# A transformer stack on one core: full-column fillers among the one-column mean-square products of three norms

## The chip, the cores and the metric

The kernel runs on one core of one Trainium2 chip. The metric is the time of one execution on the device in microseconds; the number given for a kernel is the median of several executions.

## The reference

The input x has 256 tokens of 1024 features, in float32. Two layers of a first block (root-mean-square norm with a modulation, a wide input projection, three kinds of attention with gates, output projections, a second norm and a residual) are followed by a second block: a norm and a recurrent/forgetting-attention mixer ("mix" 0), a norm and a feed-forward part ("ffn" 0), a norm and a gated linear attention ("mix" 1), a norm and a mixture of experts ("ffn" 1), and a last norm. What matters here is the norm, which stands at every one of these joints:

```
def rms_norm(x, g):
    xf = x.astype(jnp.float32)
    y = xf * lax.rsqrt(jnp.mean(xf * xf, axis=-1, keepdims=True) + EPS)
    return (y * g.astype(jnp.float32)).astype(x.dtype)
```

## The kernel before

x lies on the chip transposed, features on the 128 partitions, in KD = 8 groups k of 128 features by S = 256 tokens; a token's mean square is therefore a sum over partitions and over k, and TensorE makes it. Each engine has its own list of instructions, written out by hand in one order, and the engines meet only at semaphores; TensorE's order is that of the code in its block.

At a norm the steps are these. VectorE finishes x, two k at a time (L2439 and L2443 after a layer of the first block, L2614 after the feed-forward part). ScalarE squares it, two k at a time, into `sq` (`pair_squares`, L1471). TensorE multiplies each square, as the stationary operand, with one column of a matrix that holds 1/1024: `token_square` (L654), two matmuls per k (one for each 128 tokens) of a single output column each, all summed in one bank of the accumulators; `token_squares` (L660) does this for all eight k, waiting before each for its square. ScalarE takes the root (L1516), VectorE the reciprocal (`inverse_tokens`, L2145), and `spread` (L667) turns the 2 columns of reciprocals into 128 equal rows over 256 tokens with two matmuls against the identity. VectorE multiplies h with them (L2313, L2472). In the projections that follow, h is needed as two parts of lower precision, upper and lower, which ScalarE (L1593, L1506) and VectorE (L2317, L2476) form; a product of two such operands is three matmuls (`product`, L693 to L698).

`keep_busy(n)` (L676) puts n matmuls of 128 by 128 by 128 into a bank of the attention group, whose result nobody reads. It waits for whatever frees the bank whose turn it is, but it claims no turn. It stands between the mean squares and the spread, where TensorE waits for the root, and between the spread and the projection, where it waits for h. A float32 matmul appears in the trace as two records.

`token_squares` is called at three places: the norm "pre" of the second layer (L896), "mix" 0 (L1014) and "mix" 1 (L1146). Elsewhere the mean squares are made between other products. After "pre" 1 comes a projection of two targets (`project`, L699 on), after "mix" 0 the forget gate's product with h (`chunk`, L643, 16 records), after "mix" 1 a product with 16 columns (the same helper).

Of the kernel before, what the change touches and what calls it, by code (L numbers as in the profile page):

```python
# [83 lines left out]
class Ticks:  # L84
# [12 lines left out]
    def when(self, sem, *step):  # L97
        return self.known.get((sem.name, *step), 1)


def two_blocks(nc, A, C, out, known):

    _, S, D = A["x"].shape
    L = A["w_in"].shape[0]
    KD, NT = D // P, S // P
    FF = A["ev_ffn_w1_2"].shape[2]
    NE, _, FE = A["od_exp_w1_2"].shape[1:]
    SLOT, RING = 2048, 6
    ticks = Ticks(known)
# [279 lines left out]
    def cols(name, l, a, b, k=None):  # L389
# [6 lines left out]
    ADA_SPREAD = {("gcols", 0, 0): (1, 2), ("gcols", 0, 3): (1, 3), ("gcols", 0, 8): (1, 1),  # L396
                  ("gcols", 1, 0): (1, 4), ("gcols", 1, 3): (1, 5)}
    ADA_UNITS = [(0, 0), (0, 1), (0, 2)] + [u for _, u in ADA_LATER.items()]
    ADA_SLOW = [u for _, u in ADA_SPREAD.items()]

# [126 lines left out]
    def wrote(*key):  # L527
        tick(psum_ready, *key)
        return 1
# [81 lines left out]
    def _(pe):  # L611
# [4 lines left out]
        def claim(group, key, freed_by, *step):  # L616

            n = order[group][turn[group] % 4]
            turn[group] += 1
            if n in busy:  # L620
                pe.wait_ge(busy[n][0], busy[n][1])
            busy[n] = (freed_by, when(freed_by, *step))
            ticks.counts[("bank", *key)] = n
            return bank[n]
# [29 lines left out]
        def token_square(b, at, tile, k, scale, start, stop):  # L654
            for t in range(NT):
                m = nc.tensor.matmul(b[:, at + t:at + t + 1], tile[:, k, P * t:P * t + P], mean[scale][:, 0:1],  # L656
                                     start=start and t == 0, stop=stop, skip_group_check=True)
            return m

        def token_squares(key):  # L660
            b = claim("gemm", ("ms", *key), rstd_ready, *key)
            for k in range(KD):
                pe.wait_ge(sq_ready, when(sq_ready, *key, k))
                m = token_square(b, 0, sq, k, 1024, k == 0, k == KD - 1)
            m.then_inc(psum_ready, wrote("ms", *key))

        def spread(key, first, n, freed_by, *step):  # L667

            pe.wait_ge(rstd_ready, when(rstd_ready, *key))
            b = claim("gemm", ("r", *key, first), freed_by, *step)  # L670
            for t in range(n):
                m = nc.tensor.matmul(b[:, P * t:P * t + P], rtok[:, first + t:first + t + 1].broadcast_to([P, P]), ident,
                                     start=True, stop=True)
            m.then_inc(psum_ready, wrote("r", *key, first))

        def keep_busy(n):  # L676

            b = order["attn"][turn["attn"] % 4]
            pe.wait_ge(*busy[b])
            for _ in range(n):  # L680
                nc.tensor.matmul(bank[b][:, 0:P], mean[1024], ident, start=True, stop=True)  # L681
# [209 lines left out]
        for l in range(L):  # L891
            if l == 0:
                for i in range(3):
                    modulation(0, i)
            else:
                token_squares(("pre", l))  # L896
                keep_busy(4)
                spread(("pre", l), 0, NT, h_ready, "pre", l, KD - 1)
                keep_busy(6)
# [112 lines left out]


        token_squares(("mix", 0))  # L1014
        keep_busy(4)
        spread(("mix", 0), 0, NT, h_ready, "mix", 0, KD - 1)
        keep_busy(5)
        pe.wait_ge(flog_spread, when(flog_spread, "all"))
        chunk(("flog",), "gemm", clog_ready, ("flog",), KD, lambda k: flogw[:, k], lambda k: h[:, k],
              fresh=("mix", 0))  # L1020
# [122 lines left out]
        for n in range(4):  # L1143
            busy[4 + n] = (x_ready, when(x_ready, "ffn", 2 * n + 1))

        token_squares(("mix", 1))  # L1146
        keep_busy(6)
        spread(("mix", 1), 0, NT, h_ready, "mix", 1, KD - 1)
# [1873 lines left out]
```

## Time and profile before

| | us |
|---|---|
| median of 3 executions | 2174.56 (2170.38 to 2179.92) |
| the profiled execution | 2178.82 |
| its span | 2177.0 |
| TensorE busy, matmuls | 2125.8 |
| VectorE busy | 1618.2 |
| ScalarE busy | 1273.3 |
| mean granted TensorE clock | 0.981 of full |

The span runs from the first to the last instruction in the profile; the device time of the same execution has 1.8 us around it. "PE" is TensorE's matmuls, "PEld" its weight loads, which overlap them. The granted clock is given as a share of 2.4 GHz, and 0.50 is the lower level, 1.2 GHz.

### The profile page before, as it was taken

To read this page: it belongs to the slowest core of one execution; us is meant where nothing else is said; L and a number is where in the kernel's file an instruction comes from. 1 tells how busy PE (TensorE), PEld (TensorE's weight loads), DVE (VectorE), ACT (ScalarE), POOL (GpSimd) and SP (SyncE) were. 2 spreads that over 40 slices of the span, in tenths; PEclk is the share of its full clock that TensorE was granted. 3 is DMA by queue.
4 is the path that set the end of the run, shared out by engine and by line. 5 is a ranking of instruction groups with operands and counts; after the bars stand their busy time and mean duration, and the time that the engine had idled before them with its cause. 6 is when DMAs were issued, how large, how long until landed. Compare 5 with 4: busy or idle time off the path is not lost.

```text
span 2177.0 us, 33231 instructions
## 1 busy us (share of the span) xinstructions
PE 2125.8 (98%) x12854; PEld 1904.0 (87%) x12854; DVE 1618.2 (74%) x1928; ACT 1273.3 (58%) x1546; POOL 26.7 (1%) x19
## 2 busy tenths in 40 slices
PE   6999999999999999999999999999999999999997
PEld 6899999999999989999998888888888888888886
DVE  6668866558855755555637888898898888888886
ACT  2645534645524744334635777777676777777675
POOL 0000000000000300000000000000000000000000
PEclk6999999999999999998999999999999999999999
DMA  9975355665435425554557999999999999999990
GB/s 287 238 239 184 120 173 118 161 188 180 117 117 171 145 88 176 190 160 140 156 189 283 374 343 353 357 347 376 334 365 341 362 347 351 376 331 368 335 352 29
DMA packets 361202, 536.48 MB, mean 246 GB/s; under 512 B 67724, under 2 KB 207936, under 8 KB 361096
## 3 DMA queue, kind: packets, MB, share of 16 engines
q1 hardware_dynamic: 355536, 530.81, 72.0%
q10 hardware_dynamic: 5560, 4.19, 0.7%
q8 instruction: 75, 1.23, 0.2%
q14 instruction: 31, 0.25, 0.0%
HBM read 533.89 MB, written 1.07 MB: 246 GB/s over the span
## 4 chain that ended last, share of the span: by engine, by line
PE 76%; DVE 3%; ACT 2%; issue 1%; DMA 0%; DVEq 0%; ACTq 0%
PE bank L696 21%; PE bank L698 21%; PE bank L697 21%; PE bank L643 3%; PE bank L1309 2%; PE bank L1264 1%; PE bank L1363 1%; ACT w_hi L1960 1%; PE bank L656 1%; PE bank L849 1%; DVE w_lo L2715 1%; PE bank L681 1%; DVE piece_lo L2452 1%; ACT piece_hi L1482 0%; PE bank L832 0%
## 5 line engine op out<-in xcount | busy, mean ns | idle before, releaser
L2715 DVE TENSOR_TENSOR w_lo<-pool,w_hi 128x2048 fp32r<-128x2048 f32 x336 | 765.1, 2292 | 101.3 <-ACT w_hi L1960 100.6
L1960 ACT ACTIVATE w_hi<-pool 128x2048 fp32r<-128x2048 f32 x336 | 643.0, 1917 | 135.4 <-PE bank L698 135.0
L696 PE MATMUL bank<-w_hi,xe_hi 128*128 128x512 f32 x896 | 356.2, 397 | 3.7 <-DVE h L2814 3.4
L698 PE MATMUL bank<-w_hi,xe_lo 128*128 128x512 f32 x896 | 349.7, 390 | 0.0
L697 PE MATMUL bank<-w_lo,xe_hi 128*128 128x512 f32 x896 | 349.1, 390 | 0.0
L696 PE MATMUL bank<-h_upper,upper 128*128 128x256 f32 x992 | 293.4, 296 | 3.2 <-DVE h_lo L2262 3.2
L697 PE MATMUL bank<-h_lo,upper 128*128 128x256 f32 x992 | 281.6, 284 | 0.0
L698 PE MATMUL bank<-h_upper,ring_lo 128*128 128x256 f32 x992 | 281.6, 284 | 0.0
L2172 DVE TENSOR_TENSOR ring_lo<-ring,upper 128x1024 fp32r<-128x1024 f32 x132 | 160.4, 1222 | 98.5 <-ACT upper L1493 98.0
L2452 DVE TENSOR_TENSOR piece_lo<-ring,piece_hi 128x1024 fp32r<-128x1024 f32 x118 | 144.9, 1236 | 100.4 <-ACT piece_hi L1482 100.1
L696 PEld LDWEIGHTS bank<-w_hi,xe_hi 128*128 128x128 f32 x896 | 168.2, 188 | 45.1 <-DVE h L2814 6.3
L698 PEld LDWEIGHTS bank<-w_hi,xe_lo 128*128 128x128 f32 x896 | 168.2, 188 | 36.1
L697 PEld LDWEIGHTS bank<-w_lo,xe_hi 128*128 128x128 f32 x896 | 168.5, 188 | 33.2
L696 PEld LDWEIGHTS bank<-h_upper,upper 128*128 128x128 f32 x992 | 190.9, 192 | 5.9 <-issue 4.1
L696 PE MATMUL bank<-left_hi,piece_hi 128*128 128x256 f32 x672 | 193.9, 289 | 0.8 <-DVE left_lo L2476 0.8
L697 PEld LDWEIGHTS bank<-h_lo,upper 128*128 128x128 f32 x992 | 191.0, 193 | 1.7 <-issue 0.2
L697 PE MATMUL bank<-left_lo,piece_hi 128*128 128x256 f32 x672 | 191.3, 285 | 0.0
L698 PE MATMUL bank<-left_hi,piece_lo 128*128 128x256 f32 x672 | 191.3, 285 | 0.0
L698 PEld LDWEIGHTS bank<-h_upper,ring_lo 128*128 128x128 f32 x992 | 190.8, 192 | 0.0
L696 PE MATMUL bank<-w_hi,hT_hi 128*128 128x512 f32 x448 | 176.0, 393 | 0.0
L698 PE MATMUL bank<-w_hi,hT_lo 128*128 128x512 f32 x448 | 174.5, 389 | 0.0
L697 PE MATMUL bank<-w_lo,hT_hi 128*128 128x512 f32 x448 | 174.3, 389 | 0.0
(396 smaller groups left out, 3427.0 us busy)
## 6 DMA issues: line engine op xcount, KB each, us to landing
pool<-in_od_exp_w SPq DMA_DIRECT2D x336, 1024.0 KB, 7.2
ring<-in_w_in SPq DMA_DIRECT2D x48, 1024.0 KB, 5.4
ring<-in_ev_ffn_w SPq DMA_DIRECT2D x33, 1024.0 KB, 5.3
ring<-in_w_ada SPq DMA_DIRECT2D x24, 1024.0 KB, 7.2
ring<-in_od_w_in SPq DMA_DIRECT2D x12, 1024.0 KB, 5.6
ring<-in_ev_w_in SPq DMA_DIRECT2D x10, 1024.0 KB, 5.4
ring<-in_w_in SPq DMA_DIRECT2D x32, 256.0 KB, 4.6
ring<-in_w_out SPq DMA_DIRECT2D x8, 1024.0 KB, 5.1
```

The lines of the kernel that those rows point to most:

```text
L643: m = nc.tensor.matmul(b[base:base + rows, 0:cols], left(k), right(k), start=(k == 0), stop=(k == K - 1))
L656: m = nc.tensor.matmul(b[:, at + t:at + t + 1], tile[:, k, P * t:P * t + P], mean[scale][:, 0:1], start=start and t == 0, stop=stop, skip_ ...
L681: nc.tensor.matmul(bank[b][:, 0:P], mean[1024], ident, start=True, stop=True)
L696: nc.tensor.matmul(b, left[0], right[0], start=first, stop=False, skip_group_check=True)
L697: nc.tensor.matmul(b, left[0], right[1], start=False, stop=False, skip_group_check=True)
L698: return nc.tensor.matmul(b, left[1], right[0], start=False, stop=last, skip_group_check=True)
L849: m = nc.tensor.matmul(b[:, 0:S], v[:, k, at:at + P], pT[:, k], start=(k == 0), stop=(k == NT - 1))
L1309: m = nc.tensor.matmul(bank[n][:, P * c:P * c + P], h_tok[:, t, P * (4 * g + c):P * (4 * g + c) + P], pick_tok[:, t], start=(t == 0), stop ...
L1960: nc.scalar.activation(w_hi[q % 3], ring_slot(q), ACT.Copy)\
L2172: V.tensor_tensor(dst, src, split(upper[:, n % PIECES], KD, P).bitcast(F32), ALU.subtract)\
L2452: V.tensor_tensor(lo, src, hi.bitcast(F32), ALU.subtract).then_inc(piece_ready, tick(piece_ready, n))
L2715: V.tensor_tensor(w_lo[q % 3], ring_slot(q), w_hi[q % 3].bitcast(F32), ALU.subtract)\
```

## The change

Inside `token_squares`, ahead of the products of k = 2, 4 and 6, three unread full-column matmuls are issued: nine per call, at three calls. And the fillers between the spread and the forget gate's product at "mix" 0 go from five to eight.

```
@@ -661,6 +661,8 @@
             b = claim("gemm", ("ms", *key), rstd_ready, *key)
             for k in range(KD):
                 pe.wait_ge(sq_ready, when(sq_ready, *key, k))
+                if k in (2, 4, 6):
+                    keep_busy(3)
                 m = token_square(b, 0, sq, k, 1024, k == 0, k == KD - 1)
             m.then_inc(psum_ready, wrote("ms", *key))
 
@@ -1014,7 +1016,7 @@
         token_squares(("mix", 0))
         keep_busy(4)
         spread(("mix", 0), 0, NT, h_ready, "mix", 0, KD - 1)
-        keep_busy(5)
+        keep_busy(8)
```

## Rows read from the trace of the kernel before

**Rows 1.** The page: span, busy time, and the chain that ended last by engine.
```profile
span 2177.0 us, 33231 instructions
...
PE 2125.8 (98%) x12854; PEld 1904.0 (87%) x12854; DVE 1618.2 (74%) x1928; ACT 1273.3 (58%) x1546; POOL 26.7 (1%) x19
...
PE 76%; DVE 3%; ACT 2%; issue 1%; DMA 0%; DVEq 0%; ACTq 0%
```

**Rows 2.** Windows around the norms: stretch, length, PE busy, PEclk, DMA share, GB/s.
```profile
366.90:371.00 4.10, 3.85 (x32) 1.00 0.00 1
...
372.10:375.40 3.30, 3.05 (x15) 0.50 0.00 0
...
679.10:682.80 3.70, 3.37 (x27) 0.98 0.54 170
682.90:689.50 6.60, 6.60 (x30) 0.50 0.39 110
...
1004.80:1006.90 2.10, 2.10 (x22) 1.00 0.03 8
1007.00:1013.70 6.70, 6.70 (x33) 0.50 0.00 0
```

**Rows 3.** Chain at "mix" 1: start us, us on the chain, what.
```profile
1004.90 4.65 PE bank L656 x32
1009.54 2.77 PE bank L681 x12
1012.31 0.85 PE bank L672 x4
1013.17 1.69 PE bank L681 x12
1014.85 3.56 PE bank L643 x16
```

**Rows 4.** Chain at "mix" 0.
```profile
681.51 2.54 PE bank L656 x16
684.05 1.92 PE bank L681 x8
685.97 0.85 PE bank L672 x4
686.82 2.13 PE bank L681 x10
688.95 3.79 PE bank L643 x16
```

**Rows 5.** Timeline at "mix" 0: start us, us, engine, line, what, [idle before <-releaser].
```profile
680.31 0.97 PEld L656 LDWEIGHTS bank<-mean,sq 128*128 128x128 f32 x8 [0.17 <-ACT sq L1471]
...
681.51 2.46 PEld L656 LDWEIGHTS bank<-mean,sq 128*128 128x128 f32 x16 [0.23 <-ACT sq L1471]
```

**Rows 6.** Timeline at "pre" 1.
```profile
368.02 0.97 PEld L656 LDWEIGHTS bank<-mean,sq 128*128 128x128 f32 x8 [0.17 <-ACT sq L1471]
...
369.22 1.86 PEld L656 LDWEIGHTS bank<-mean,sq 128*128 128x128 f32 x16 [0.23 <-ACT sq L1471]
...
371.06 1.22 DVE L2172 TENSOR_TENSOR ring_lo<-ring,upper 128x1024 fp32r<-128x1024 f32 x1
...
374.99 0.88 DVE L2317 SCALAR_TENSOR_TENSOR h_lo<-h,small,h_upper 128x256 fp32r<-128x256 f32 x2
```

**Rows 7.** One-column products amid other work: the chain, and the window around it.
```profile
620.75 1.68 PE bank L656 x16
...
618.00:624.20 6.20, 6.20 (x38) 5.68 (x37) 1.90 (x5) 1.74 (x3) 0.00 (x0) 1.00 0.52 169
```

**Rows 8.** Chain at "pre" 1.
```profile
372.41 1.22 PE bank L672 x4
373.63 2.27 PE bank L681 x12
```

**Rows 9.** Window after "mix" 1: length, five engines' busy time, PEclk, DMA share, GB/s.
```profile
1024.00:1031.00 7.00, 7.00 (x32) 6.35 (x31) 1.31 (x2) 1.73 (x5) 0.00 (x0) 0.51 0.83 260
```

More of the change, by code:

```diff
@@ L663, in token_squares @@
                 pe.wait_ge(sq_ready, when(sq_ready, *key, k))
+                if k in (2, 4, 6):
+                    keep_busy(3)
                 m = token_square(b, 0, sq, k, 1024, k == 0, k == KD - 1)
@@ L1016, in _ @@
         spread(("mix", 0), 0, NT, h_ready, "mix", 0, KD - 1)
-        keep_busy(5)
+        keep_busy(8)
         pe.wait_ge(flog_spread, when(flog_spread, "all"))
```

## The prediction

> **What bounds the kernel now.** I read the page first: the shares of busy time and the chain that ended last. TensorE (PE) is busy for 98% of a 2177.0 us span and carries 76% of the chain; no other engine has more than 3% [rows 1]. So a microsecond added to or taken from PE's own order counts in full, unless PE stands waiting at that point. Then I cut the span into short windows and looked at the granted clock around the three norms that the diff touches ("pre" of layer 1, "mix" 0, "mix" 1). In each the clock goes from 1.00 to 0.50, the lower of its two levels (1.2 GHz where 2.4 is full), and stays there: about 3.3 us at pre 1, 6.7 us at mix 0, 6.8 us at mix 1 [rows 2]. What PE did just before is the same each time: the one-column products of `token_square`. The reader should see that PE was not idle: 2.10 us busy in 2.10 us before the fall at mix 1, 3.37 in 3.70 at mix 0, 3.85 in 4.10 at pre 1 [rows 2]. Last, the chain and the timeline of each place show what each instruction costs at either level and who waits for whom.
>
> **Prices.** One fp32 matmul is two records. A one-column record costs 0.105 us at full clock (16 in 1.68 us [rows 7]); at half clock 0.21: of the 32 at mix 1, some 19.7 fit at 0.105 between 1004.90 and the fall near 1006.97, and the other 12.3 take the remaining 2.57 us [rows 3]. A full-column filler record costs 0.141 at full clock (12 in 1.69) and 0.231 at half (12 in 2.77) [rows 3]. So a group of three fillers (6 records) costs 0.85 or 1.39 us, four fillers 1.13 or 1.85, and a pair of k (8 one-column records) 0.84 or 1.68. The spread (4 records) costs 0.85 at half [rows 3, 4] and, at the filler's price, 0.56 at full.
>
> **The change, part by part.** It adds three fillers before k = 2, 4 and 6 in each of three calls: 27 matmuls, 54 records, 7.6 us of PE at full clock, 12.5 at half. And `keep_busy(5)` becomes `keep_busy(8)` at mix 0: 6 more records, 0.85 us. Nothing is removed. The fillers wait for no one: at all three places the bank they write is bank 4 of the attention group (68 claims a layer, and 16 between the mixes, all multiples of four), and what frees it has happened; at mix 1 that is the first pair of x, which must be there before the first square can be made. They do sit in front of the real products, behind which ScalarE's root waits, then VectorE's reciprocal, the spread, and all products with h.
>
> Whether the clock then holds decides what they give back. PE now never goes longer than about 1.2 us without a full-column matmul (at mix 0 from the end of the fillers near 679.1, where a window of [rows 2] begins, to the first new group at 680.31 [rows 5]), and 0.84 us between groups. The trace has sixteen one-column records, 1.68 us, amid full-column work with the clock at 1.00 throughout [rows 7], and the falls came after runs of some 2 to 4 us of them [rows 2]. I take it that the clock holds.
>
> Mix 0. The squares of k = 2, 3 release PE at 680.31, and the next pair would come 1.2 us later [rows 5]; with 1.69 us of work per pair PE is now the slower side. Three times 0.85 + 0.84 from 680.31 puts the end of the mean squares at 685.38, where it was 681.51 + 2.54 = 684.05 [rows 4]: 1.33 us later. Four fillers at full clock: 686.51 (was 685.97). Spread: 687.07 (was 686.82). Eight fillers, 2.26 us: 689.3 (was 688.95). The forget-gate product of 16 records then needs 3.56 us at full clock (its like at mix 1 [rows 3]) where it took 3.79: 692.9 against 692.74. Net +0.2 us: what the clock gives, the fillers take.
>
> Mix 1. Here all squares are ready and PE runs through. From 1004.90: four pairs and three groups, 4 x 0.84 + 3 x 0.85 = 5.9, to 1010.8 (was 1009.54). Six fillers 1.69: 1012.5 (1012.31). Spread: 1013.0 (1013.17). Six fillers: 1014.7 (1014.85) [rows 3]. Unrounded the 32 records are 3.36, so net -0.2 us, within 0.1.
>
> Pre 1. PE was released at 368.02 and at 369.22 [rows 6]; from 368.02, 3 x 1.69 gives 373.09 for the end of the mean squares, where it was 369.22 + 1.68 = 370.90: 2.2 us later. Part was hidden: VectorE's reciprocal came only behind a piece subtraction started at 371.06 that took 1.22 us [rows 6]. Four fillers: 374.22; spread: 374.8 (was 372.41 + 1.22 = 373.63 [rows 8]), 1.15 later. The first half of h came at 374.99 + 0.44 = 375.43 [rows 6] and now comes at 376.6; six fillers end at 376.5. The projection began at 375.90 [rows 8] and now begins at 376.6: +0.7 us.
>
> Sum: 0.7 + 0.2 - 0.2 = +0.7 us. Bounds: the clock falls as before and the fillers cost all they can, +8.4 us (first rival); every half-clock stretch disappears at no cost for the fillers, (3.3 + 6.7 + 6.8) / 2 = -8.4 us. I take the middle because the steps above can be followed record by record. The profiled execution took 2178.82 us, 1.8 beyond its span; with the change 2179.5. The median of the runs is 2174.56, 4.3 below it, and the same 0.7 us on the median gives 2175.3, which I predict.
>
> The windows before the falls bear on one rule. The Trainium skill ("TensorE: Matmul & The Clock Gate", section "Why this matters for your kernels") ties a drop of the clock in mid-kernel to idle gaps of PE between bursts of matmuls. By that rule fillers put where PE is busy anyway would keep nothing, and the sum would be that of the first rival; the trace disagrees, since at mix 1 the clock fell with PE busy 2.10 of 2.10 us.
>
> **Rivals.**
> 1. *The clock falls all the same* (slower). Place: the same three norms; it decides if one-column products mixed with fillers still count as they do alone. Then the fillers past the fall cost 1.39 a group. Pre 1, fall near 372.05, back near 375.5: mean squares end 374.1, spread 376.3, 2.7 later than before, projection at 378.1: +2.2. Mix 0, fall near 682.84, back near 689.6: groups and pairs end at 687.6, four fillers 689.4, spread 690.1, eight fillers 692.35, gate product 695.9: +3.2. Mix 1, fall at 1006.97, back at 1013.8: mean squares 1013.9, spread 1016.2, fillers 1017.9 against 1014.85: +3.0. Together +8.4: 2183. For it: at mix 0 the clock stayed at 0.50 through eight filler records on end (684.05 to 685.97) [rows 4], so fillers do not act at once. Against: rows 7.
> 2. *It holds, and the runs gain more than the profiled one would* (faster). In this execution each half-clock stretch happens to end just as the projections start. Where it lies later it covers products at double price; a stretch of 3.3 us over serial work costs 1.65 us, up to 5 us over three places: 2170. For it: the runs of the kernel before differ by 9.5 us. Against: nothing ties that spread to this. (The Trainium skill, same page, section "What's actually happening", says that the point of the change of clock moves from run to run; one execution cannot show it.)
> 3. *A later fall goes too* (faster). From 1024 to 1031 the clock is at 0.51 [rows 9], behind mix 1's small low-rank product; if shifted work spares that, half of some 6.4 us is won: -3.2, 2172. Nothing in the diff feeds that stretch, so I give it little.
> 4. *It holds at one or two places only*: between +0.7 and +8.4, about +4, 2178.6.
>
> **How the numbers follow.** Forecast 0.50; the clock falls everywhere 0.12; in part 0.16; gain beyond the profile 0.15; the later fall goes 0.07. A run of this kernel can tell about 0.5%, 10.9 us, from no change, and neither bound reaches that: +8.4 is 0.39%. Only the spread of the runs themselves (2170.38 to 2179.92) can carry a median over the line, a little more readily on the slow side: slower 0.05, faster 0.04, within 0.91. The range takes in rivals 2 and 3, most of 4, and the runs' own scatter of a few us: 2169 to 2181.5.
>
> **What would show it.** Right: 210 filler records where there were 150 (75 + 30 matmuls, two records each); granted clock 1.00 through all three norms; mean squares ending 1 to 2 us later after their first square, but fillers and spreads at 0.141 a record. Wrong: 0.50 still standing in any of the three, with groups of six records at 1.39 us (rival 1 or 4); a projection that starts earlier than before, measured from the first square; or a change of more than 3 us in a stretch outside these norms.

## The result, and the profile after

The changed kernel took 2186.49 us in the median of 9 executions (2178.84 to 2186.97), the kernel before 2175.54 (2170.38 to 2179.92): a ratio of 1.0040, 95% interval 1.0027 to 1.0054, so it is slower by 6 to 12 us. The prediction was 2175.3 with 2169 to 2181.5 around it. The profiled execution took 2186.30.

Its page, for [rows 1]:

```profile
span 2184.5 us, 33360 instructions
...
PE 2129.7 (97%) x12914; PEld 1907.6 (87%) x12914; DVE 1617.1 (74%) x1928; ACT 1273.7 (58%) x1546; POOL 26.7 (1%) x19
```

PE has 60 more records, the 30 fillers, and 3.9 us more busy time; the span grew by 7.5. So about half of the loss in this pair of profiles is PE standing still.

The windows around the three norms, for [rows 2] (stretch, length, PE busy, PEclk, DMA share, GB/s):

```profile
366.80:369.80 3.00, 2.89 (x24) 1.00 0.01 1
370.00:380.10 10.10, 10.10 (x49) 0.50 0.01 2
683.60:692.60 9.00, 8.85 (x78) 1.00 0.23 69
1010.40:1019.30 8.90, 8.90 (x81) 1.00 0.00 0
1026.40:1030.70 4.30, 0.00 (x0) 0.77 1.07 348
1029.00:1038.40 9.40, 7.63 (x26) 0.50 0.59 188
```

Two of the three norms went as forecast, at 1.00 throughout. At pre 1 the clock fell although fillers had begun, and it stayed at 0.50 for 10.1 us where it had stayed 3.3. The last two windows are of a place that the diff does not touch: behind mix 1 PE does nothing for 4.3 us, and a half-clock stretch of 10.2 us follows, of which the last window shows 9.4; before it was 6.8.

The chain at pre 1, for [rows 8], shows the prices in both states:

```profile
367.93 0.94 PE bank L683 x6
368.86 0.79 PE bank L656 x8
369.65 1.10 PE bank L683 x6
370.75 1.50 PE bank L656 x8
372.25 1.49 PE bank L683 x6
373.74 1.50 PE bank L656 x8
375.23 1.92 PE bank L683 x8
377.15 0.85 PE bank L674 x4
378.00 2.44 PE bank L683 x12
```

A group and a pair cost 0.9 + 0.8 us before the fall and 1.5 + 1.5 after it. The spread is at 377.15, where it was at 372.41.

Behind mix 1, the timeline of the kernel before (start us, us, engine, line, what, [idle before <-releaser]):

```profile
1018.43 0.45 ACTq L1437 DMA_DIRECT2D pool<-in_od_gate_w  x1
1018.44 3.29 SPq L2955 DMA_DIRECT2D ring<-in_od_w_in  x3
1022.55 1.31 PE L643 MATMUL bank<-pool 16*128 16x256 f32 x5 [1.09 <-ACT pool L1525]
```

and of the changed one:

```profile
1023.26 3.64 SPq L2957 DMA_DIRECT2D ring<-in_od_w_in  x3
1023.29 1.71 ACTq L1439 DMA_DIRECT2D pool<-in_od_gate_w  x1
1030.77 0.76 PE L643 MATMUL bank<-pool 16*128 16x256 f32 x1 [4.49 <-issue]
```

`od_gate_w` is a load of 32 KB, the weights of the small gate product (L1161) that PE does after one more projection; ScalarE issues it, and in front of that product PE waits for it and for two other small loads (`loaded_gla`). Beside it SyncE issues three loads of 1 MB. The DMA view gives the time from issue to landing, before:

```profile
pool<-in_od_gate_w ACTq DMA_DIRECT2D x1, 32.0 KB, 4.0
```

and after:

```profile
pool<-in_od_gate_w ACTq DMA_DIRECT2D x1, 32.0 KB, 7.4
```

1023.29 + 7.4 is 1030.7, the moment at which PE goes on; the profile calls the releaser "issue" because it ties no DMA to the wait. PE idle for 4.49 us in place of 1.09 is 3.4 us, nearly all of the loss that is no busy time.

### The profile page after: what moved, and what is told of

Same layout as the page of the kernel before. It is cut to its first block, busy times and chain, and to the rows that moved or that the text cites. A ratio compares the mean times of both kernels' runs of the same rounds, so it can differ in the third digit from the quotient of the medians.

```text
span 2184.5 us, 33360 instructions
## 1 busy us (share of the span) xinstructions
PE 2129.7 (97%) x12914; PEld 1907.6 (87%) x12914; DVE 1617.1 (74%) x1928; ACT 1273.7 (58%) x1546; POOL 26.7 (1%) x19
## 4 chain that ended last, share of the span: by engine, by line
PE 91%; DVE 3%; ACT 3%; issue 2%; DMA 1%; ACTq 0%; DVEq 0%
PE bank L698 24%; PE bank L700 24%; PE bank L699 24%; PE bank L643 5%; PE bank L851 2%; PE bank L1311 2%; PE bank L1266 1%; PE bank L656 1%; PE bank L1365 1%; ACT w_hi L1962 1%; PE bank L683 1%; PE bank L834 1%; DVE w_lo L2717 1%; PE bank L820 1%; PE bank L824 1%
```

## The experiments

A norm's cost is read as the time from one root on ScalarE (L1516 in the kernel before) to the next that lies well behind it. The profile has such a root at 362.71 and 614.55 (stage A, with pre 1), 675.00 and 808.26 (stage B, with mix 0), 808.26 and 1095.12 (stage C, with mix 1 and the loads behind it). Every run below has a profile, so these can be set side by side (us; "held" and "fell" are PEclk in the norm; "load" is issue to landing of the gate weights):

```
                    A: pre 1         B: mix 0         C: mix 1         load
no fillers in the stage
before              251.84 fell      133.26 fell      286.86 fell      4.0
before_again        253.78 fell      135.27 fell      288.56 fell      5.7
before_gate_early   253.80 fell      131.93 fell      281.55 fell      early
pre_only                             133.26 fell      281.60 held      4.5
mix0_only           251.83 fell                       281.72 fell      2.5
mix1_only           253.72 fell      135.24 fell
mix1_gate_early     252.23 fell      135.30 fell
groups of three in the stage
after               256.40 fell      134.05 held      290.56 held      7.4
after_again         252.53 held      137.26 fell      289.78 held      6.0
after_gate_early    252.51 held      137.40 fell      282.32 held      early
after_loads_behind  252.52 held      137.50 fell      282.37 held      3.0
pre_only            256.58 fell
mix0_only                            137.28 fell
mix1_only                                             284.49 held      4.3
mix1_gate_early                                       281.95 held      early
```

All runs have 11 or 12 timed executions, but for the ones where it is said; the times of one kernel spread over 3 to 15 us (those of the kernel before over 10 to 15 in each set), so an edit of 1 or 2 us is read in the stages.

**pre_only**, the fillers at one norm:

```
-                if k in (2, 4, 6):
+                if k in (2, 4, 6) and key == ("pre", 1):
```
(against the changed kernel, with five fillers at mix 0 as before)

> The kernel before with the nine fillers at 'pre' of layer 1 alone. Theory (the fillers there do not hold the clock, and they push the mean squares and everything behind them through a stretch at half clock): the granted clock falls to 0.50 while they run, the stretch is some 10 us instead of 3.4, and the root at the next norm comes about 4.5 us later than in the profile before; time +4 to +5 us. Rival A (the fall was an accident of that one execution): the clock holds in this profile and the norm costs +0.7 us, as first predicted. Rival B (the whole loss of the change sits in the late DMA wait behind mix 1): about +1 us here, unless the wait flips by itself. If the gate weights' load behind mix 1 still beats the three large loads, PE waits about 1.2 us there as before, not 4.5.

Measured: 2173.65 us, ratio 0.9991 (0.9983 to 1.0000). Its profile has the clock at 0.50 for 10.2 us and stage A at 256.58, 4.7 over the profile before, as the theory said:

```profile
369.40:379.60 10.20, 10.20 (x49) 0.50 0.01 2
1019.70:1031.00 11.30, 9.73 (x71) 1.00 0.96 298
```

But the time is not longer. The second row is the place behind mix 1: here no half-clock stretch followed, and stage C took 281.60 instead of 286.86. The profile of the kernel before was a dear one at C, and its median holds both sorts. The theory's stretch is there; its time is wrong.

**mix0_only** (`key == ("mix", 0)`, eight fillers behind the spread):

> The kernel before with the nine fillers at 'mix' 0 alone and eight instead of five behind the spread. Theory: the clock holds at 1.00 there and the norm costs +0.8 to +1.1 us from the root before it to the root after it (the fillers take what the clock gives); total within 1 us of the kernel before, unless the race of the loads behind mix 1 flips. Rival (the fillers hold the clock only by luck of phase): 0.50 appears in this profile at mix 0 and it costs +3 us.

Measured: 2176.68 us, ratio 1.0004 (0.9991 to 1.0016). The rival's stretch came: 0.50 for 10.1 us, stage B 137.28, +4.0.

```profile
681.30:691.40 10.10, 10.10 (x50) 0.50 0.25 75
```

So the hold at mix 0 in the first profile of the changed kernel was one case out of two.

**mix1_only** (`key == ("mix", 1)`):

> The kernel before with the nine fillers at 'mix' 1 alone. Theory (race of loads): the clock holds through the norm, the 16-column product now ends as soon as h is there, SyncE's three loads of 1 MB go out just ahead of ScalarE's load of the 32 KB gate weights, that load lands 7 us after its issue instead of 4, and PE waits some 4.5 us in front of the gate product instead of 1.2: +3 to +4 us although the norm itself gets 0.4 us shorter. Rival (the long wait was an accident of one execution, not tied to the change): the wait stays near 1.2 us in this profile and the time is -0.4 us or the same.

Measured: 2177.22 us, ratio 0.9998 (0.9986 to 1.0010). The clock held, and SyncE's loads went out at 1021.74 ahead of ScalarE's at 1021.78, yet the small one landed after 4.3 us. Which of the two is issued first, by a few hundredths, does not decide; that part of the theory fell.

**after_gate_early**, the small loads moved up in ScalarE's list (the root waits for the same mean squares):

```
         token_root("mix", 1)
+        fetch(loaded_gla, w2lr[0:16, :], A["od_gate_w2_2"][0])
+        fetch(loaded_gla, chunkmask, C["chunkmask"])
+        fetch(loaded_gla, restart, C["restart"])
         pair_uppers(("mix", 1))
...
-        act.wait_ge(psum_ready, when(psum_ready, "ms", "mix", 1))
-        fetch(loaded_gla, chunkmask, C["chunkmask"])
-        fetch(loaded_gla, restart, C["restart"])
-        fetch(loaded_gla, w2lr[0:16, :], A["od_gate_w2_2"][0])
```

> The changed kernel with the three small loads of the gated linear attention (gate weights first) issued by ScalarE straight behind the root of mix 1, ahead of forming the upper parts of h, instead of behind them. Theory (race of loads): the loads land some 4 us before PE needs them, the wait in front of the gate product shrinks from 4.5 us to below 1.5, and with it most of the half-clock stretch behind it: -4 to -6 us against the changed kernel, so about +3 to +5 against the kernel before. Rival (the wait is not the loads): no change, +8 to +11 against before.

Measured: 2179.08 us, 7.4 below the changed kernel's 2186.49 and with a ratio of 1.0003 (0.9990 to 1.0016) to the kernel before. Stage C falls from 290.56 to 282.32. The window over the place where PE had stood:

```profile
1022.90:1033.00 10.10, 10.10 (x76) 1.00 0.95 297
```

PE is busy without a break, and the clock does not fall here. So most of the loss goes with the late load. The median is still 3.5 us above that of the kernel before in the same set of runs (2175.62), which the interval allows.

**after_again** and **before_again**, both kernels unaltered, for second profiles (`before_again` was timed once):

> The changed kernel once more, unaltered, for a second profile and a second set of times. Theory (the change has no fixed cost; it depends on where the fall of the clock can land): at each of pre 1 and mix 0 the clock either holds, then the norm costs +0.7 to +0.8 us over the kernel before, or falls for about 10 us, then +4 to +4.6; at mix 1 it holds. The time lies anywhere from 2175 to 2187. And the gate weights' load behind mix 1 lands 2.5 to 4.5 us after its issue, as in the four other profiles, or, as in the first profile of this kernel, 7.4. Rival (that long load belongs to this kernel): it lands after some 7 us again, PE waits some 4.5 us, and the time is 2184 to 2187 again.

> The kernel before once more, unaltered, for a second profile. Theory: its half-clock stretches move against the norms: at pre 1 one of 3.4 or 6.8 us, at mix 0 6.8 us, at mix 1 none, 3.4 or 6.8; the stage from the root of ffn 0 to the first root of the gated attention takes between 281.6 and 286.9 us. Rival: the same stretches as in its first profile (3.4, 6.8, 6.8), 286.9 us.

Measured: 2185.37 us for the changed kernel, ratio 1.0027 (1.0010 to 1.0043). At pre 1 the clock now held (A 252.53), at mix 0 it fell (B 137.26): exchanged against the first profile. The load landed after 6.0 us. The single execution of the kernel before took 2186.83 us, as long as the changed one's median, and shows all four stretches and the late load too:

```profile
370.00:376.80 6.80, 6.77 (x31) 0.50 0.00 0
684.00:690.80 6.80, 6.65 (x31) 0.50 0.04 8
1011.70:1018.50 6.80, 6.80 (x33) 0.50 0.00 0
1028.80:1035.50 6.70, 6.58 (x21) 0.50 0.85 268
```

The stretches are among those that the theory allowed; stage C, at 288.56, lies above what theory and rival had. So the late load is no property of the changed kernel: it is an event that both have. Of all 125 executions of the kernel before, 21 took more than 2180 us; of the 21 of the changed kernel 17 did. Only the profiled ones show whether a long time goes with the late load.

**before_gate_early** and **mix1_gate_early**, the early loads without fillers and with those of mix 1 alone:

> The kernel before with the three small loads behind mix 1 issued straight behind the root, gate weights first. Theory: the load is there when PE asks; the time from the end of the 16-column product to the gate product goes from 3.3 to 4.6 us to about 2.9: -1 us in the usual case, up to -4 where the load would have been late. Rival (the wait is no part of the end): same time as before, within 0.5 us.

> The fillers at mix 1 alone, where the clock held in three of three profiles, and the early loads; nothing at pre 1 and mix 0, where it fell in two of three each. Theory: -0.4 us at the norm on the average and -1 us or more at the loads: 1 to 3 us faster than the kernel before, the fastest of all. Rival (the fillers at mix 1 give nothing): the same as the early loads alone.

Measured: 2174.19 us, ratio 0.9995 (0.9984 to 1.0006), and 2175.13 us, ratio 0.9993 (0.9982 to 1.0004). Both medians are 1 to 2 us below the kernel before timed beside them (2176.32), and both intervals hold 1. Neither is shown to beat it. With the second of them, fillers of three per group had held the clock at mix 1 in all five profiles so far.

`before_gate_early` is also the kernel to set `after_gate_early` against, since both have the early loads and only one the fillers: 2179.08 is 4.9 us above 2174.19 by the medians, and by the ratios to the kernel before it is 1.7 us. The two were timed in different sets of runs, so that is a rough measure of what the fillers at the norms cost by themselves.

**delay_5**, **delay_5_gate_early**: 18 fillers on end ahead of the mean squares of pre 1 (`keep_busy(18)` before `token_squares(("pre", l))`), the second with the early loads:

> The kernel before with 18 full-column fillers on end (5.1 us at full clock) ahead of the mean squares of pre 1 and nothing else: a plain delay, as large as what the fillers of the change cost in their profiles (+4.5 us). Some of it is hidden, since PE waits there: +3.5 to +5 us arrive behind pre 1. Theory (amplified delay): whatever makes the program reach the loads behind mix 1 later than some 1023 us meets a slow load of the gate weights (landing 5.7 to 7.4 us after issue instead of 2.5 to 4.5) and a half-clock stretch behind it, so that the time is +8 to +11 us, as for the changed kernel. Rival (a delay is only a delay; the late loads have another reason): +3.5 to +5 us, 2179 to 2181, and the load lands within 4.5 us.

> The same plain delay with the three small loads issued straight behind the root of mix 1. Theory (amplified delay): without the wait for the load only the delay itself is left, +3 to +4.5 us against the kernel before, and 4 to 7 us less than with the loads where they were. Rival: the same as with the loads where they were, less 1 us.

Measured: 2176.05 us, ratio 0.9997 (0.9986 to 1.0009), and 2177.34 us, ratio 1.0004 (0.9995 to 1.0013). Most of the delay vanished, against theory and rival: stage A took 253.98 and 254.54, 1.1 and 1.7 us over the average of 252.9 of the six profiles without fillers there (251.8 to 253.8), although the block is 5.1 us. In the first the clock held at pre 1 through the block and the 3.5 us of one-column products behind it; in the second it fell for 3.4 us. Since mix 1 was not reached late (the load was issued at 1020.73 and landed after 3.9 us), the pair says nothing of the late load.

**dense_gate_early**, groups of six instead of three at the three norms, early loads:

> Six fillers instead of three in each group at all three norms (five behind the spread at mix 0), and the early loads. Theory (three per group are too few among the one-column products for the clock to hold in every position): with twice as many no granted clock of 0.50 appears between the first square and the projection at any of the three norms; nine more fillers a norm cost 2.5 us each, so pre 1 and mix 0 take +3.2 and about +2.5 us over the kernel before instead of +0.7 or +4 to +4.6, mix 1 some +2; time +7 to +8 us, 2182 to 2184. Rival (fillers between one-column products cannot hold the clock, however many): 0.50 appears at one of pre 1 and mix 0 again.

Measured: 2180.21 us, ratio 1.0013 (1.0004 to 1.0023).

```profile
367.30:378.00 10.70, 10.61 (x92) 1.00 0.01 2
684.50:696.00 11.50, 11.38 (x88) 1.00 0.27 80
1011.00:1020.00 9.00, 9.00 (x82) 1.00 0.09 27
```

Held at all three, in one profile. Stage A took 254.55, B 134.41: 3.0 less at B than a fall with groups of three (0.85 of it because only five fillers stand behind the spread here, not eight), 2.0 more at A than a hold. The time is 2 us below the forecast of 2182 to 2184, and the kernel is slower than before nevertheless: these fillers cost more than the fall that they replace.

**delay_ffn_7**, **delay_ffn_14**: 24 and 49 more fillers in front of the spread of ffn 0 (`keep_busy(30)` and `keep_busy(55)` for `keep_busy(6)`; the second was timed in 6 executions):

> The kernel before with 30 full-column fillers instead of 6 ahead of the spread of ffn 0: a plain delay of some 6.8 us right before the feed-forward part, so that the loads behind mix 1 are issued at 1025 to 1030 us instead of 1018 to 1023. Theory (the load of the gate weights is slow whenever it is issued later than about 1023 us, as in the first and second profile of the changed kernel and the second of the kernel before): it lands 5.7 us or more after its issue, and the time is +10 us or more. Rival (the late landing has nothing to do with the time of issue): it lands within 4.5 us, and the time is +6 to +7 us.

> The same with 55 fillers: +13.8 us of delay. Theory: slow again, the landing 5.7 us or more after the issue, +17 us or more. A variant of it (the slow landing belongs to a band of times and not to a threshold): within 4.5 us again, and the time is 13 to 14 us above the kernel before, about 7 above delay_ffn_7 or even less. Rival: 13 to 14 above before and exactly 7 above delay_ffn_7, and both land fast.

Measured: 2182.20 us, ratio 1.0031 (1.0018 to 1.0043), and 2186.16 us, ratio 1.0045 (1.0029 to 1.0061). The load was issued at 1022.39 and landed after 2.5 us in the first, at 1028.58 and after 4.5 us in the second. A later issue is not a slower load: the theory of a threshold fell with the second. The first delay costs what it is, 6.9 us over the 2175.32 of the kernel before timed beside it; the second costs 10.8 of its 13.8, 4.0 more than the first where the rival had 7, and what took the other 3 was not looked into.

**after_loads_behind**, SyncE holds the large loads back:

```
                 sp.wait_ge(*freed_at[n - RING])
+            if n == where[("lr",)] + RING:
+                sp.wait_ge(loaded_gla, when(loaded_gla, "all"))
             for tile, src in copies:
```

> The changed kernel in which SyncE holds back the three 1 MB loads behind mix 1 until ScalarE's small loads have landed. Theory (the gate weights wait behind the three large loads): they land within 3 us of their issue, PE waits 1 us or less more than with the early loads, and the large loads come some 3 us later, which PE does not notice or only by 1 or 2 us: -4 to -7 us against the changed kernel, 2178 to 2181. Rival (the load is slow for itself): it lands 5.7 us or more after the issue again and the time is 2184 to 2188.

Measured: 2178.13 us, ratio 1.0005 (0.9992 to 1.0017), 7.2 and 8.4 below the two medians of the changed kernel and 2.8 above the kernel before in the same set of runs. The timeline, against the one above, and the DMA view:

```profile
1023.58 1.61 ACTq L1439 DMA_DIRECT2D pool<-in_od_gate_w  x1
1026.64 0.99 SPq L2959 DMA_DIRECT2D ring<-in_od_w_in  x2
1026.65 0.88 PE L643 MATMUL bank<-pool 16*128 16x256 f32 x3
...
pool<-in_od_gate_w ACTq DMA_DIRECT2D x1, 32.0 KB, 3.0
```

Even an issue that took 1.61 us, as in the changed kernel's first profile, now lands after 3.0 us, PE goes on at 1026.65 instead of 1030.77, and the window behind has no fall:

```profile
1022.00:1040.00 18.00, 17.80 (x133) 1.00 0.79 242
```

Two different edits, one that issues the small load earlier and one that issues the large ones later, take some 7 us away. That the large loads make the gate weights late in the changed kernel, and that this wait with the half-clock stretch behind it makes up most of the loss, is shown.

## Why the prediction was wrong, step by step

**The time and the place.** The sum of +0.7 us was for three norms; by the medians most of the loss lies behind the third, where I had priced nothing. The step that failed is "Nothing is removed. The fillers wait for no one" taken as the whole account, and with it "Nothing in the diff feeds that stretch" in rival 3, on just the place of the loss: what the fillers shift was put at nothing. Measured from the end of the 16-column product to the root that closes stage C, that place took 1104.08 - 1023.23 = 80.85 us against 1095.12 - 1018.41 = 76.71: +4.1 of the 9.0 us between the two profiles up to there, though the kernel before had a fall there too [rows 9]. It is also the sign of being wrong that the prediction named, more than 3 us outside the norms. By the medians it is the 7 to 8 of 11 us that either cure takes away. The other failed step, that the clock holds, gave +4.6 us at pre 1.

The wait itself was there to be seen. PE's wait in front of the gate product was already bound by a load. The chain of the kernel before shows it as "issue" between the row of the 16-column result and the product:

```profile
1021.50 0.39 ACT pool L1525
1021.89 0.66 issue
1022.55 2.33 PE bank L643 x8
```

Its load was issued at 1018.43 and took 4.0 us, to 1022.4, and a load that is only just in time in a race with three large ones was a risk that the profile showed. Take it away and the changed kernel is at 1.0003 or 1.0005 of the kernel before, both intervals holding 1: with that, the forecast of no measurable change for the edit itself is not refuted, though by the medians 2.8 and 3.5 us are left.

**"I take it that the clock holds."** Wrong as a rule. With groups of three it held at mix 1 in 6 of 6 profiles, at pre 1 in 3 of 5, at mix 0 in 1 of 5. Without fillers it fell at pre 1 and mix 0 in every profile (but at pre 1 of `delay_5`, with its block of 18 in front), and at mix 1 it fell in 7 of 9, all but `pre_only` and `delay_5`. The difference between the places fits what PE does beforehand, though no run tests it: at mix 1 it comes out of the projections without a pause, at the others it waits for the first squares [rows 5, 6]. My argument, sixteen one-column records amid full-column work at 1.00 [rows 7], was of such a place.

**Where it held, the sums were right.** Stage A 252.51 to 252.53 against 251.84: +0.7, as worked out, though in part by luck: against the 252.9 that the profiles without fillers average it is -0.4. Stage B 134.05 against 133.26: +0.8, forecast +0.2; but that stage B also holds a fall of 3.4 us near 735, far behind the norm, as do those with 135.2 to 135.3, against which it is 1.2 us faster. Mix 1, from the root of ffn 0 to the end of the 16-column product: 1023.23 - 813.52 = 209.71 against 1018.41 - 808.26 = 210.15: -0.4, forecast -0.2 (the steps of the forecast, added up, give -0.1).

**Where it fell, rival 1 was too low.** It had the stretch as long as before, and +2.2 and +3.2 us. The fall lasted 10.1 or 10.2 us every time in place of 3.4 or 6.8, and cost +4.6 to +4.7 at A and +4.0 to +4.2 at B against the first profile, +3.6 and +3.3 (on the average) against the averages without fillers. The prices at half clock were near enough: 1.5 us a group and 1.5 a pair for 1.39 and 1.68. Eight filler records on end at half clock (375.23 to 377.15) did not bring the clock back; it came back while the fillers behind the spread ran, as it had before the change. What ends a fall is not shown.

**The baseline.** I worked against one profile as if it were the kernel. Its pre 1 was among the cheapest (251.84 where others have up to 253.80) and its mix 1 dear (286.86 where the others without the late load have 281.6 to 284.5). Over the profiles of the table the stages with fillers average 254.1 (five profiles) against 252.9 without (six) at A, 136.7 (five) against 134.0 (six) at B: together about 4 us, which fits the medians of the kernels with either cure for the load (+2.8 and +3.5 us), but their intervals also allow nothing.

**The bound.** "neither bound reaches that" (+8.4 us being 0.39%) let me put 0.05 on slower. A bound from the touched instructions alone bounds the touched instructions, not the kernel.

**The rule on idle gaps.** Behind mix 1 PE was idle from 1026.3 and the clock fell near 1028.7, and stayed up in both kernels where the idle time went. There the rule of the Trainium skill ("TensorE: Matmul & The Clock Gate", "Why this matters for your kernels"), that idle gaps between bursts bring the clock down, and the trace agree. In the norms the clock fell with PE busy, as said above; the rule alone does not cover them.

**Open.** Why the event is so frequent in the changed kernel (its two profiles of two, 17 of 21 executions) and rare in the one before. Which of the two engines issues first by a few hundredths decides nothing (ScalarE came first in `before_again`, 1023.18 against 1023.20, and was late; second in `mix1_only`, and was not), nor does the time of issue by itself. A longer lead goes with a fast load: where SyncE's first large load came 0.29 and 0.69 us behind the small one (`mix0_only`, `delay_ffn_7`) it landed after 2.5 us, where the two came within 0.04 us of each other, in eight profiles, after 3.9 to 7.4. In two profiles ScalarE's issue itself took 1.6 and 1.7 us instead of 0.45; it is not known why. `after_again` and `before_again` had the late load without that.

One lead stands in the traces. In all three profiles of the changed kernel with the small loads at their old place (`after`, `after_again`, `after_loads_behind`), the DMA view of the 2.5 us from ScalarE's first small load on has a transfer of instructions on queue q8. In `after`, from 1022.42 to 1024.92:

```profile
q8 instruction: 1, 0.02, 3.4%
```

In the 2.5 us from the first small load on, none of the other 13 profiles has one. In these three the two small loads ahead of the gate weights also landed later, after 2.1 to 2.4 and 3.1 to 3.3 us in place of 1.8 to 2.0 and 2.1 to 2.4, even with the large loads held back. So the place of that transfer, which would move with the number of TensorE's instructions, may be what makes the event frequent; that is a guess, no run varied it alone, and `before_again` was late without it.

## What to carry to other kernels

Before adding work to a critical engine, look behind the edit for waits that end just in time, small loads beside large ones above all; either of two cures (small load earlier, large loads behind it) took some 7 us off the changed kernel here. Fillers between one-column products won no time here: groups of three held the clock in 10 of 16 cases, and where it fell the stretch was 10.2 us in place of 3.4 or 6.8; groups of six held it in three of three, and the kernel was slower than before. Where a kernel's times spread over 10 us, profile the kernel before twice, and compare stages.

## What the runs showed of the hardware

The clock fell with TensorE busy all the time (2.10 of 2.10 us [rows 2]) and stayed at 0.50 through groups of fillers among one-column products for 10.1 to 10.2 us, in all six falls with groups of three at pre 1 and mix 0. A load of 32 KB with no large load beside it landed after 1.7 us (in all five profiles with the early loads); beside three loads of 1 MB, the first of them issued within 0.7 us of it, after 2.5 to 7.4. The Trainium skill ("Trainium Kernel Development and Optimization", "Key Constraints") says that transfers issued by different engines run on the same 16 DMA engines and interleave; the runs agree so far as the small load landed after 6.0 and 7.4 us beside the large ones in the changed kernel and after 3.0 with them held back.
